# A hybrid decoder trunk on one core: smaller first operands on two queues, two products interleaved, unread products ahead of them, and a tile of values moved to the first stage

## What is computed

```
z = x @ w_in                      # (512, 1024) @ (1024, 3*512 attention + 3*512+64+64+128 RWKV columns)
zs = z_rwkv + (shift(z_rwkv) - z_rwkv) * mu          # r, k, v and three small inputs (decay, iclr, gate)
o_rwkv  = rwkv7_time_mix(zs)                          # a recurrence over the tokens, 8 heads of 64
o_att   = moba_attention(z_att)                       # 8 heads of 64, causal, ALiBi
x = LN(alpha*x + [o_att | o_rwkv] @ w_out)
x = LN(alpha*x + cross_attention(x, mem))
x = LN(alpha*x + top-2-of-32-experts(x))              # w_gate, w_up, w_down of each expert: 6 MB
```

## Time and profile before

| | us |
|---|---|
| median of 3 runs | 1171.56 |
| the profiled execution's own time | 1172.06 |
| its span, first to last instruction | 1170.5 |
| TensorE busy | 1045.2 (89%) |
| VectorE busy | 328.5 (28%) |
| ScalarE busy | 245.7 (21%) |
| mean granted TensorE clock | 0.972 |

### The profile page before, as it was taken

How to read it: one execution, slowest core, us unless ns; L and a number is a source line. 1 busy time by engine, 2 the same in 40 slices (tenths; PEclk the granted TensorE clock), 3 DMA queues, 4 the chain that set the end, 5 groups by cost and what they waited for, 6 DMA issues and landing times. The chain is left out here.

```text
span 1170.5 us, 15693 instructions
## 1 busy us (share of the span) xinstructions
PE 1045.2 (89%) x6602; PEld 522.7 (45%) x6602; DVE 328.5 (28%) x709; ACT 245.7 (21%) x498; POOL 84.5 (7%) x131
## 2 busy tenths in 40 slices
PE   7999899999898999999896699999997777788895
PEld 3444455567655544566344344444433333333332
DVE  0179622234565463005136200000000000000007
ACT  2341122234453501014202111111111111011112
POOL 2000100000000000000100211111111101110100
PEclk9999899999999999999998699999999999998998
DMA  6112220222024310903216699999999999999994
GB/s 237 43 62 86 95 73 2 73 74 74 2 73 145 120 61 6 353 4 141 113 72 234 260 406 407 408 405 400 397 399 389 401 390 384 398 401 402 394 413 185
DMA packets 55382, 262.83 MB, mean 225 GB/s; under 512 B 7170, under 2 KB 8322, under 8 KB 30352
## 3 DMA queue, kind: packets, MB, share of 16 engines
q1 hardware_dynamic: 50048, 253.39, 55.9%
q0 software_dynamic: 5120, 8.40, 2.2%
q10 hardware_dynamic: 144, 0.02, 0.0%
HBM read 257.60 MB, written 12.58 MB: 231 GB/s over the span
## 5 line engine op out<-in xcount | busy, mean ns | idle before, releaser
L2114 PE MATMUL cpair<-ring,xgT 128*64 128x512 f32 x352 | 79.0, 594 | 11.2 <-DMA ring<-in_w_exp_up 10.5
L2311 DVE TENSOR_TENSOR hs<-cpair,hs 64x512 f32<-64x512 f32 x21 | 14.6, 693 | 263.4 <-ACT hs L2241 263.4
L2124 PE MATMUL bank<-ring,hT 128*64 128x512 f32 x240 | 57.9, 627 | 7.7 <-DVE hT L2315 7.7
L901 PE MATMUL bank<-xT,ring 128*128 128x512 f32 x128 | 60.3, 605 | 0.0
L2047 POOL DMA_INDIRECT y_rows<-ye,tabs x30 | 29.9, 998 | 390.8 <-ACT ye L2247 390.8
L2114 PE MATMUL tpair<-ring,xgT 128*64 128x512 f32 x192 | 45.2, 616 | 9.1 <-DMA ring<-in_w_exp_up 7.6
L2114 PEld LDWEIGHTS cpair<-ring,xgT 128*64 128x64 f32 x352 | 25.9, 137 | 61.3 <-issue 60.4
L2247 ACT ACTIVATE ye<-bank,tabs 128x512 f32<-128x512 f32 x30 | 20.6, 687 | 148.2 <-PE bank L2124 148.2
L2311 DVE TENSOR_TENSOR hs<-tpair,hs 64x512 f32<-64x512 f32 x11 | 7.6, 693 | 147.6 <-ACT hs L2241 147.6
L346 PE MATMUL bank<-xT,ring 128*128 128x512 f32 x112 | 48.5, 593 | 0.0
L2241 ACT ACTIVATE hs<-cpair 64x512 f32<-64x512 f32 x21 | 12.3, 588 | 160.0 <-PE cpair L2114 160.0
(11 more groups left out here) (427 smaller groups left out, 1730.3 us busy)
## 6 DMA issues: line engine op xcount, KB each, us to landing
ring<-in_w_exp_gate SPq DMA_DIRECT2D x34, 1024.0 KB, 10.9
ring<-in_w_exp_up SPq DMA_DIRECT2D x34, 1024.0 KB, 10.8
ring<-in_w_exp_down SPq DMA_DIRECT2D x32, 1024.0 KB, 11.2
ring<-in_w_in SPq DMA_DIRECT2D x6, 2048.0 KB, 8.0
ring<-in_w_mem_kv SPq DMA_DIRECT2D x4, 2048.0 KB, 10.2
xT<-in_w_exp_down SPq DMA_DIRECT2D x8, 1024.0 KB, 10.7
xT<-in_w_exp_gate SPq DMA_DIRECT2D x6, 1024.0 KB, 10.9
xT<-in_w_exp_up SPq DMA_DIRECT2D x6, 1024.0 KB
```

The costliest lines, as they stand in the source:

```text
L901: last = nc.tensor.matmul(dst[:, :], lhs, rhs, start=(k == 0), stop=(k == KT - 1))
L2114: last = nc.tensor.matmul(bank[b][m * CAP:(m + 1) * CAP, :], xgT[:, k, :], w(m, h)[:, j * DE:(j + 1) * DE], start=(k == 0), stop=(k == KT ...
L2124: last = nc.tensor.matmul(bank[b][m * CAP:(m + 1) * CAP, :], ht[:, k, :], w(2, h)[:, o:o + 512], start=(k == 0), stop=(k == FT - 1))
L2311: V.tensor_tensor(hb, bank[1 + e % 3][CAP:P, :], sil, ALU.mult).then_inc(h_done, 1)
```

## The change

- The first operands come in four parts over k (k = 0; 1; 2 and 3; 4 to 7). The tokens go on SyncE's queue, the weights on ScalarE's, ahead of `cols`. TensorE does L0 and L1 side by side, both products of a k before the next k, into banks 0 and 1; each part has a semaphore that counts both transfers.
- Ahead of them TensorE does `WARM` = 8 products ident x ident (128x128x128) into bank 7, which nobody reads; it waits for `ident`.
- `cen` is computed by GpSimd at the end of its constants in the first stage, and the wait for it goes.
- `AV_EARLY` is 3: tile AV2 is done in the first stage, and 80 units are left before round 30. `fill_at` spreads them evenly: 2 units in every third round and 3 in the others, where before it was 3 in rounds 0 to 28 and 1 in round 29.

```diff
-                x_here = [part_sem(f"x_here{i}") for i in range(2)]
-                gl_half = part_sem("gl_half")
+                first_ks = [slice(0, 1), slice(1, 2), slice(2, 4), slice(4, KT)]
+                x_here = [part_sem(f"x_here{i}") for i in range(len(first_ks))]
+                ident_done = part_sem("ident_done")
...
-                AV_EARLY = 2
+                AV_EARLY = 3
+                WARM = 8
...
-                        gl = slot(GL, 2 * P)
-                        for h, (here, done) in enumerate(((x_here[0], gl_half), (x_here[1], w_here[slot_of(GL)]))):
-                            ks = slice(4 * h, 4 * h + 4)
-                            sp.dma_start(gl[:, ks, :], groups[GL][:, ks, :]).then_inc(done, 16)
+                        for ks, here in zip(first_ks, x_here):
                             sp.dma_start(xT[:, ks, :], x_t[:, ks, :]).then_inc(here, 16)
                         load_group(sp, GK)
...
                             pool.wait_ge(consts_done, h + 1)
+                        link(pool, pool.tensor_scalar(cen[:, :], blkones[:, :], -1.0 / HD, None, ALU.mult))
+                        pool.wait_ge(ident_done, 1)
+                        link(pool, pool.tensor_tensor(cen[:, :], cen[:, :], ident[:, :], ALU.add))
...
                     def _(pe):
+                        pe.wait_ge(ident_done, 1)
+                        for n in range(WARM):
+                            nc.tensor.matmul(bank[7][:, 0:P], ident[:, :], ident[:, :], start=True, stop=True)
+                        w = slot(GL, 2 * P)
+                        for k in range(KT):
+                            for ks, here in zip(first_ks, x_here):
+                                if ks.start == k:
+                                    pe.wait_ge(here, 16 if here is x_here[-1] else 32)
+                                    if here is x_here[-1]:
+                                        group_here(pe, GL)
+                            for j in range(2):
+                                last = nc.tensor.matmul(bank[j][:, :], w[:, k, j * P:(j + 1) * P], xT[:, k, :],
+                                                        start=(k == 0), stop=(k == KT - 1))
+                                if k == KT - 1:
+                                    last.then_inc(job_full, 1)
                         for n, (kind, j) in enumerate(jobs):
+                            if kind == "L":
+                                continue
...
                     def _(act):
+                        gl = slot(GL, 2 * P)
+                        for ks, here in zip(first_ks, x_here[:-1] + [w_here[slot_of(GL)]]):
+                            act.dma_start(gl[:, ks, :], groups[GL][:, ks, :]).then_inc(here, 16)
                         act.dma_start(cols[:, :], params).then_inc(cols_here, 16)
...
-                fill_at = ([min(3 * r, early_units) for r in range(MS)]
+                fill_at = ([early_units * r // MS for r in range(MS)]
...
-                        pe.wait_ge(cen_done, 1)
...
-                        link(dve, V.tensor_scalar(cen[:, :], blkones[:, :], -1.0 / HD, None, ALU.mult))
-                        V.tensor_tensor(cen[:, :], cen[:, :], ident[:, :], ALU.add).then_inc(cen_done, 1)
```

More of the change, by code:

```diff
@@ L222, in hybrid_decoder_trunk @@
             twice = sa("twice", [P, CH])
+            cen = sa("cen", [P, P])
             A1 = ExitStack()
@@ L301, in _ @@
                         pool.affine_select(out=ident[:, :], in_=ident[:, :], compare_op=ALU.not_equal,
-                                           fill=1.0, base=0, pattern=[[-1, P]], channel_multiplier=1)
+                                           fill=1.0, base=0, pattern=[[-1, P]], channel_multiplier=1)\
+                            .then_inc(ident_done, 1)
                         link(pool, pool.memset(base3[:, :, :, :], 0.0))
@@ L334, in _ @@
                         for n, (kind, j) in enumerate(jobs):
+                            if kind == "L":
+                                continue
                             dst = bank[n % 8]
                             wait_bank_free(pe, n)
[L337 to L341, removed]
+                            if kind in ("K", "R", "V"):
+                                g = {"K": GK, "R": GR, "V": GV}[kind]
+                                w = slot(g, 512)
+                                group_here(pe, g)
@@ L342, in _ @@
                                 for k in range(KT):
-                                    if n == 0 and k % 4 == 0:
-                                        pe.wait_ge(gl_half, 16) if k == 0 else group_here(pe, g)
-                                        pe.wait_ge(x_here[k // 4], 16)
                                     last = nc.tensor.matmul(dst[:, :], w[:, k, j * P:(j + 1) * P], xT[:, k, :],
@@ L494, in hybrid_decoder_trunk @@
                 memT = s2("memT", [P, KT, MEM])
-                cen = s2("cen", [P, P])
                 dist = s2("dist", [P, 512])
@@ L517, in hybrid_decoder_trunk @@
                 orm = osq
-                loop_consts, cen_done, mem_here = part_sem("loop_consts"), part_sem("cen_done"), part_sem("mem_here")
+                loop_consts, mem_here = part_sem("loop_consts"), part_sem("mem_here")
                 units_done = part_sem("units_done")
```

## The result

| | before | after |
|---|---|---|
| median of the runs (4 each), us | 1171.33 | 1158.97 |
| lowest and highest | 1170.42 to 1172.59 | 1158.13 to 1162.98 |
| ratio, with its 95% interval | | 0.9918 [0.9899, 0.9937] |
| the profiled execution's own time / span | 1172.06 / 1170.5 | 1159.28 / 1157.7 |
| TensorE busy, mean granted clock | 1045.2, 0.972 | 1047.5, 0.971 |

The change makes the kernel faster. The ratio puts it at 1171.56 x 0.9918 = 1162.0 us, 9.6 us less; the bare medians stand 12.4 apart. The same kernel run again (further down) gave 0.9931 and 1161.39. So the size is 8 to 10 us by the two estimates (7.4 to 11.8 by the interval of the first), and the 12.8 between the two profiled spans is more than the change earns. Where the rest comes from is part of what the experiments look for.

The account below looks back on a forecast made before the run. TensorE was taken to set the pace up to round 30, with everything behind, expert-weight stream included, moving along. Terms: 2.6 - 4.2 + 3.0 + 6.9 = 8.3 us; 1171.56 - 8.3 = 1163.3 us, range 1160.3 to 1167.5.

Parts of the forecast that it names:

- The bound and the place where to read it: First two stages: time saved there moves everything behind, expert-weight stream included; read at round 30's start, 8.3 us earlier.
- Start, 2.6: First operands: split parts and unread products bring K0 from 24.25 to 21.6, 2.6 us gained.
- By packets: Start: queues share packet by packet, so the third part lands at 10.4 us and the last at 14.7.
- Rival 1: Start: queues share by bytes, parts come in time, gain 4.2 instead of 2.6 us; 1161.7 us, chance 0.25.
- Boundary, -4.2: Between the stages: AV2 moved ahead delays the second stage's first product from 131.57 to 135.8, 4.2 us lost.
- Clock, +3.0: Behind the stage boundary: TensorE's pause shrinks from 3.77 to 1.1 us, the clock should not fall, 3.0 us gained.
- Rounds, +6.9: First 30 rounds of the second stage: eight units leave, 6.9 us gained if TensorE still ends each round.
- Rival 2: Rounds of two units end on VectorE and ScalarE, 3.4 us of gain missing; 1166.7 us, chance 0.12.
- the distance of round 30: Round 30 about 8 us earlier, the same distance still there at the chain's first long DMA piece.
- Rival 3: Start: first part no earlier or unread products delay real ones, start gain 0; 1165.9 us, chance 0.10.
- Rival 4: Thinner rounds: pauses at their ends let the clock fall; with 30 us at half clock 1178.3 us, chance 0.03.

Follow-up runs that it names:

- e11: The kernel before, run once more unchanged for a second trace; 1169.62 us, ratio 1.0003.
- e1: Against the kernel after: one queue, all four parts of weights and tokens in turn on SyncE's; 1160.16 us, ratio 0.991 to the kernel before.
- e3: Against the kernel after: AV_EARLY = 2, tile AV2 back in the second stage's rounds; 1164.28 us, ratio 0.9948 to the kernel before.
- e7: Against the kernel after: two unread products of 128x512 (1.7 us) added ahead of AV0; 1163.72 us, ratio 0.9947 to the kernel before.
- e12: Against the kernel before: four unread products of 128x512 added behind AV1, in the pause between the stages; 1166.85 us, ratio 0.998.
- e4: Against the kernel after: `cen` computed by VectorE at the head of the second stage again; 1163.89 us, ratio 0.9949 to the kernel before.
- e6: Against the kernel after: 80 units spread by the old table, three a round until used up, none in rounds 27 to 29; 1163.77 us.
- e2: Against the kernel after: the eight unread products at the start left out; 1159.5 us, ratio 0.9916 to the kernel before.
- e8: Mixed queues, against the kernel after: two small weight parts on ScalarE's queue, large ones on SyncE's between tokens; 1159.7 us, 0.9921 to the kernel before.
- e10: The same kernel as e8, run again for a second trace; 1159.51 us, ratio 0.9922 to the kernel before.

## Why the prediction was right, step by step

**The bound and the place where to read it** held. Round 30 moved by 8.5 us (7.5 against e11), forecast 8.3, and the stream of expert weights moved with it. The forecast of 1163.3 is 1.3 above the 1162.0 that the ratio gives and 1.9 above the repeat's median; its range, 1160.3 to 1167.5, holds both, while the first median of 1158.97 lies below it.

**Start, 2.6: measured 2.65.** By packets the third part was to land at 10.4 and the last at 14.7; they landed at 10.2 and 14.5, and K0 stands at 21.60 for 21.6. Rival 1 is out. The Trainium skill (DMA: Bandwidth & Descriptors, "Queues, rings and completion order") has each DMA engine go round the queues packet by packet, and the trace agrees (372 packets of one queue beside 370 of the other between 10 and 13 us). The Trainium skill's rule on the same page that a second issuing engine saves only the time of issuing ("Issuing engines are not separate DMA queues") spoke against the second queue, and e1 bears it out at K0 (0.9 us earlier with one queue), though not in the time. Three inner numbers of this step were off without harm: an unread pass took 0.22 us and not 0.26, the products ended at 5.1 and not 5.75, and the weight loads were 0.43 apart from about 5.2 instead of 6.85. TensorE thus reached the third part earlier and waited longer (1.55 us for 0.7). That the term came out to a tenth is in part luck. Against e11 the gain at K0 is only 1.65, since there the first operands came 0.3 us earlier and the weight loads stood 0.43 us apart from 11.7 and not 13.1. Kernels with the start of the change (after, e3 to e7) had K0 at 21.41 to 21.76 four times and, where the clock fell behind the wait for the third part, at 22.89 and 22.99; those with the start of before had it at 23.25, 24.25 and 24.37. The means are 1.9 us apart.

**Boundary, -4.2.** The first product of the second stage was to stand at 135.8 - 2.6 = 133.2, and stands at 132.96; the pause is 0.93 for 1.1. The barrier took 0.25 for 0.31.

**Clock, +3.0.** The clock held. e3 (3.1) and e12 (2.6) give its price from both sides of the change. That it would hold for AV2's sake was right; that a pause of 0.93 us was needed for it was not known, and e4 with 2.38 shows that a longer one can do too.

**Rounds, +6.9.** From products(0) to round 30 e3 and the change differ by 10.0, which are 6.9 and 3.1. The slack read from one level of round 2 was enough for every round that keeps two units. Rival 2 has its mechanism (e6) but only in rounds that keep none.

**The step that failed** is the sentence that the distance of round 30 would still be the same at the first long DMA piece. It was 12.8 there (840.46 against 827.63). The prediction had looked for low clock up to 250 us and in one window after, and took what lay behind for equal. It wasn't: the kernel before lost about 1.5 us at 313 and 3.0 at 466, the kernel after nothing. The 3.0 are chance, by e11. The 1.5 are not clear: behind the same pause of about 1.8 us both traces of before fell, both of the change held, both of the mixed kernel fell, and one-queue fell while e2, e3, e4, e6, e7 and e12 held. At this place each kernel that was traced twice did the same twice, but three pairs are few: with falls in five of thirteen traces they would agree by chance about once in seven. e8, e10 and e1, which come early, fell, but so did before, which comes latest. Whether this 1.5 us belongs to the change or is chance too stays open.

**Rival 3** (no gain at the start) is out by K0 in both traces of the change; e4 and e7 show that a fall of the clock there leaves only 0.3 us against e11. **Rival 4** would have needed pauses at rounds' ends; there are none before round 30, and the new table is the reason.

## What to carry to other kernels

Follow an early edit to the first stage whose start it moves, and add the terms there: four terms of 2 to 7 us came out within a few tenths each in the first pair of traces, where TensorE had no gap between them. Split first operands so that the large, late parts aren't left on the queue with the small packets (2 us at K0 in e8, none that the time shows), and expect what is won to end in the next wait (e2) or behind the next pause (e8). Before a gain of a microsecond or two is believed, profile both kernels twice: one low stretch of the clock, 3.0 us in one trace of the kernel before, was as large as a term of the sum.

## What the runs showed of the hardware that was not expected

- **A pause of 1.8 to 2.4 us may bring TensorE's clock down or leave it.** It went to 0.50 behind 2.31 us (e3), 1.77 (e8, e10, e1 and e11), 1.78 and 1.79 (before, at 313 and 466) and 2.03 and 2.16 (e7 and e4, at the start), and stayed behind 2.38 (e4), 1.78 (after, at 304), 1.75 (e12) and 1.81 (after, ahead of 455.88). Both traces of before fell behind 3.77 and 3.78 us. A fall cost between 1.3 and 3.1 us. Among pauses as near to each other as 1.77 and 1.78 both outcomes stand, so more than the length decides, and the runs don't show what.
- **The windows read a granted clock of 1.00 from the program's start,** although the weight loads come 0.85 us apart; up to the first rise only the spacing tells the level. A later fall they do show (0.50 at 12 to 15 us in e4 and e7). Passes of 128 columns took 0.22 us at the start and 0.13 at full clock.
- **Two queues share by packets, not by bytes:** 372 and 370 packets, 0.37 and 0.76 MB, between 10 and 13 us of the kernel after.
- **Eight parts of 128 KB to 1 MB on one queue moved slowly:** 231 to 255 GB/s between 4 and 7 us (e1), against 357 to 443 with transfers of 512 KB to 1 MB (before), and 359 to 370 with the two smallest weight parts on the other queue (e8). An issue took about 0.43 us, but 2 MB had been issued by 4.1 us, so issuing alone isn't the reason, and the runs don't show which it is.
